# Attention in a two-layer trunk: the values attended in two passes with the halves of v side by side, and five lower weight halves made by accumulating DMAs

## The reference, cut to what matters

```python
q, k, v = jnp.split(h @ w_qkv, 3, axis=-1)
# z = q.k / sqrt(64); mask: key strictly before query
log_keep = jnp.where(mask, -jax.nn.softplus(z), 0.0)
suffix = lax.cumsum(log_keep, axis=3, reverse=True) - log_keep
a = jnp.where(mask, jnp.exp(jax.nn.log_sigmoid(z) + suffix + log_rem[..., None]), 0.0)
acc = acc + jnp.einsum("bhts,bhsd->bhtd", a, vblk)      # "the values attended"
return acc @ w_o
```

## Time and profile before

| | us |
|---|---|
| three runs | 1867.5, 1869.03, 1880.59 |
| median | 1869.03 |
| profiled execution, its own time | 1876.87 |
| its span in the trace | 1875.1 |
| PE / DVE / ACT / POOL busy in the span | 1834.6 / 1413.6 / 916.7 / 489.2 |

### The profile page before, as it was taken

The page is one execution under the profiler, slowest core; times in us unless marked ns, Lnnn a source line. Parts: engine busy times, 40 slices in busy tenths (PEclk is TensorE's granted clock), DMA queues, the critical chain, the costliest instruction groups (busy, mean ns, idle before and its releaser), DMA issues.

```text
span 1875.1 us, 29407 instructions
## 1 busy us (share of the span) xinstructions
PE 1834.6 (98%) x11801; PEld 1644.6 (88%) x11801; DVE 1413.6 (75%) x1309; ACT 916.7 (49%) x1110; POOL 489.2 (26%) x383
## 2 busy tenths in 40 slices
PE   6999999999999999999999999999999999999998
PEld 6999988887789999888999988888888889999886
DVE  7789876589888888765798885654766698988753
ACT  6455543355275555444545453435555475454442
POOL 3343302200023443001443310321333233432021
PEclk8999999999999999999999999999999999999999
DMA  8787632232268886436787732232111287776321
GB/s 226 182 221 179 172 122 90 75 94 67 80 152 185 214 183 168 130 101 132 185 202 189 190 124 90 79 96 62 46 45 45 68 182 191 189 190 158 112 90 45
DMA packets 228826, 250.94 MB, mean 134 GB/s; under 512 B 7844, under 2 KB 196336, under 8 KB 228224
## 3 DMA queue, kind: packets, MB, share of 16 engines
q1 hardware_dynamic: 179232, 195.58, 33.4%
q0 software_dynamic: 49392, 54.08, 18.5%
q10 hardware_dynamic: 112, 0.03, 0.0%
HBM read 241.27 MB, written 2.10 MB: 130 GB/s over the span
## 4 chain that ended last, share of the span: by engine, by line
PE 81%; DVE 10%; issue 4%; ACT 2%; POOL 2%; DMA 1%; DVEq 0%; ACTq 0%; POOLq 0%
PE ps L604 36%; PE ps L400 13%; PE ps L401 13%; PE ps L402 13%; DVE y L1833 2%; DVE w_lo L1540 2%; PE ps L933 2%; PE ps L912 1%; PE ps L918 1%; DVE rinv L1530 1%; DVE w_lo L1511 1%; POOL chain L2163 1%; DVE hid L1593 1%; ACT w_hi L1035 1%; DMA hid<-hid 0%
## 5 line engine op out<-in xcount | busy, mean ns | idle before, releaser
L1540 DVE TENSOR_TENSOR w_lo<-stage,w_hi 128x1024 fp32r<-128x1024 f32 x264 | 384.2, 1467 | 31.4 <-ACT w_hi L1073 31.0
L604 PE MATMUL ps<-xs_hi,w_hi 128*128 128x256 f32 x2464 | 339.9, 279 | 11.8 <-ACT w_hi L1073 10.2
L604 PE MATMUL ps<-xs_hi,w_lo 128*128 128x256 f32 x2464 | 338.6, 279 | 6.8 <-DVE w_lo L1540 6.7
L604 PE MATMUL ps<-xs_lo,w_hi 128*128 128x256 f32 x2464 | 338.2, 279 | 2.8 <-DVE xs_lo L1751 2.2
L604 PEld LDWEIGHTS ps<-xs_hi,w_hi 128*128 128x128 f32 x2464 | 309.2, 189 | 15.0 <-issue 14.7
L604 PEld LDWEIGHTS ps<-xs_hi,w_lo 128*128 128x128 f32 x2464 | 308.3, 189 | 8.2 <-DVE w_lo L1540 8.2
L604 PEld LDWEIGHTS ps<-xs_lo,w_hi 128*128 128x128 f32 x2464 | 308.2, 188 | 3.8 <-DVE xs_lo L1751 2.8
L400 PE MATMUL ps<-xs_hi,w_hi 128*128 128x512 f32 x704 | 278.4, 395 | 0.0
L401 PE MATMUL ps<-xs_lo,w_hi 128*128 128x512 f32 x704 | 278.2, 395 | 0.0
L402 PE MATMUL ps<-xs_hi,w_lo 128*128 128x512 f32 x704 | 278.2, 395 | 0.0
L1673 DVE TENSOR_TENSOR xs_lo<-hid,xs_hi 128x1024 fp32r<-128x1024 f32 x88 | 110.5, 1256 | 177.5 <-ACT xs_hi L1192 177.4
(11 more groups left out here) (241 smaller groups left out, 2736.6 us busy)
## 6 DMA issues: line engine op xcount, KB each, us to landing
stage<-in_w_ffn_up_dram SPq DMA_DIRECT2D x88, 512.0 KB, 4.5
stage<-in_w_ffn_gate_dram SPq DMA_DIRECT2D x88, 512.0 KB, 5.2
stage<-in_w_ffn_down_dram SPq DMA_DIRECT2D x88, 512.0 KB, 3.8
chain<-in_w_ffn_gate_dram POOLq DMA_DIRECT2D x47, 512.0 KB, 6.2
stage<-in_w_ffn_gate_dram POOLq DMA_DIRECT2D x44, 512.0 KB, 8.3
chain<-in_w_ffn_up_dram SPq DMA_DIRECT2D x43, 512.0 KB, 7.1
stage<-in_w_qkv_dram SPq DMA_DIRECT2D x24, 512.0 KB, 4.8
stage<-in_w_in_ab_dram SPq DMA_DIRECT2D x16, 512.0 KB, 4.6
```

The source lines that it names most:

```text
L604: mm = pe.matmul(ps[:, bank + BANK_OF[item], t * HS:(t + 1) * HS], w[:, slot, (2 * k + t) * P:(2 * k + t + 1) * P], xs[:, PART_OF[item], k ...
L1540: dve.tensor_tensor(w_lo[:, slot, :], src, w_hi[:, slot, :].bitcast(F32), ALU.subtract).then_inc(item_lo_made, 1)
```

## The change

v is kept in one tensor `v_cat` in which the 64 upper and the 64 lower columns of a head lie side by side. attend takes these 128 columns as its weights and makes two passes, one with prob_hi and one with prob_lo. Rows 0 to 63 of bank 7 then hold the product with the upper half of v, rows 64 to 127 that with the lower half (the product lower by lower, which was left out before, comes with it). ACT moves one half to the rows of the other in `sq` (`o_moved`), and DVE adds the two into `o_att` (`add_o`, which now signals `o_copied`), behind prob_lo in its iteration.

For chunks 7 to 11 DVE's subtraction goes. In even iterations 2 to 10 ACT writes -w_hi to `w_lo` (`negate`), and in odd iterations 3 to 11 POOL issues a DMA that adds `stage` to it in SBUF (`add_lower`, 1 MB). `lower_ready` is the wait for a chunk's lower half, by either way. `project` makes its 24 matmuls in the order of the three parts, and asks for the lower half ahead of the third. Line numbers behind @@ are those of the kernel before and after; split_v on ACT and the waits of the first projections change in the same manner as what is shown.

```diff
@@ -83,6 +83,9 @@
+ADDED = tuple(range(C_ATT + 7, C_ATT + 12))
 PE_TILE = CT - 1
...
@@ -187,8 +190,7 @@
             o_att = sb("o_att", [P, DT, S], scope=att_scope)
-            v_hi = sb("v_hi", [P, TT, D], F32R, att_scope)
-            v_lo = sb("v_lo", [P, TT, D], F32R, att_scope)
+            v_cat = sb("v_cat", [P, TT, HEADS, 2, DH], F32R, att_scope)
         mixer_scope.close()
...
@@ -335,6 +340,13 @@
+        def lower_ready(engine, c):
...
+            if c in ADDED:
+                engine.wait_ge(w_lo_added[c % 2], 16 * sum(1 for other in ADDED if other <= c and other % 2 == c % 2))
+            else:
+                engine.wait_ge(w_lo_made, sum(1 for other in range(c + 1) if other not in ADDED))
...
@@ -390,6 +402,11 @@
+        def o_split(j):
...
+            both = v_cat[:, :, 2 * j:2 * j + 2].rearrange("p t h a c -> p t (h a c)")
+            return both[:, :, 0:P], both[:, :, P:2 * P]
...
@@ -422,7 +439,7 @@
                     sp.wait_ge(w_hi_made, c - 1)
-                    sp.wait_ge(w_lo_made, c - 1)
+                    lower_ready(sp, c - 2)
...
@@ -872,14 +889,17 @@
                 slot = (n // 2) % 2
-                pe.wait_ge(w_lo_made, c0 + 5 + n // 2)
+                pe.wait_ge(w_hi_made, c0 + 5 + n // 2)
                 if n == 2:
...
                     pe.wait_ge(proj_scaled, n)
-                for k in range(DT):
-                    mm = three(pe, ps[:, 6, :], *tile(slot, (n % 2) * DT + k), xg_hi[:, k, :], xg_lo[:, k, :],
-                               start=(k == 0), stop=(k == DT - 1))
+                for part in range(3):
+                    if part == 2:
+                        lower_ready(pe, c0 + 4 + n // 2)
+                    for k in range(DT):
+                        mm = pe.matmul(ps[:, 6, :], tile(slot, (n % 2) * DT + k)[part // 2], (xg_lo if part == 1 else xg_hi)[:, k, :],
+                                       start=(part == 0 and k == 0), stop=(part == 2 and k == DT - 1), skip_group_check=True)
...
@@ -922,28 +942,26 @@
-                j = h // 2
                 pe.wait_ge(prob_hi_made, h + 1)
...
                     pe.wait_ge(o_copied, h)
-                for n, (v, part) in enumerate(((v_hi, prob_hi), (v_lo, prob_hi), (v_hi, prob_lo))):
-                    if n == 2:
+                for n, part in enumerate((prob_hi, prob_lo)):
+                    if n == 1:
                         pe.wait_ge(prob_lo_made, h + 1)
                     for b in range(TT):
-                        mm = pe.matmul(ps[:, 7, b * P:S], v[:, b, j * P:(j + 1) * P],
+                        mm = pe.matmul(ps[:, 7, b * P:S], v_cat[:, b, h].rearrange("p a c -> p (a c)"),
                                        part[:, KEY_OFF[b]:KEY_OFF[b] + KEY_COLS[b]], start=(n == 0 and b == 0),
-                                       stop=(n == 2 and b == TT - 1), skip_group_check=True)
+                                       stop=(n == 1 and b == TT - 1), skip_group_check=True)
                 mm.then_inc(att_summed, 1)
...
                 n, k0 = q // 4, 4 * (q // 8)
-                pe.wait_ge(w_lo_made, c0 + 13 + n)
+                lower_ready(pe, c0 + 12 + n)
                 for k in range(k_from, k_to):
                     pe.wait_ge(o_lo_made, k0 + k + 1)
-                    cols = slice((k0 + k) * P, (k0 + k + 1) * P)
                     mm = three(pe, ps[:, bank, :].rearrange("p (t c) -> p t c", t=TT), *tile(n % 2, 4 * k + q % 4),
-                               v_hi[:, :, cols], v_lo[:, :, cols], start=(k == 0), stop=(k == 3))
+                               *o_split(k0 + k), start=(k == 0), stop=(k == 3))
                 if k_to < 4:
...
@@ -1339,6 +1357,13 @@
             c0 = C_CONV
+            def negate(c):
...
+                slot = slot_of(c)
+                act.wait_ge(w_hi_made, c + 1)
+                act.activation(w_lo_c[:, slot, :], w_hi_c[:, slot, :].bitcast(F32), ACT.Copy,
+                               scale=-1.0).then_inc(w_neg_made, 1)
...
@@ -1441,8 +1466,7 @@
                 act.wait_ge(o_copied, 2 * j + 2)
-                act.activation(v_hi[:, :, j * P:(j + 1) * P], o_att[:, j, :].rearrange("p (t c) -> p t c", t=TT),
-                               ACT.Copy).then_inc(o_hi_made, 1)
+                act.activation(o_split(j)[0], o_att[:, j, :].rearrange("p (t c) -> p t c", t=TT), ACT.Copy).then_inc(o_hi_made, 1)
...
@@ -1472,14 +1496,16 @@
                     act.wait_ge(att_summed, h - 1)
-                    r = slice(DH * (h % 2), DH * (h % 2) + DH)
-                    act.activation(o_att[r, (h - 2) // 2, :], ps[r, 7, :], ACT.Copy).then_inc(o_copied, 1)
+                    r, other = slice(DH * (h % 2), DH * (h % 2) + DH), slice(DH - DH * (h % 2), P - DH * (h % 2))
+                    act.activation(sq[r, :], ps[other, 7, :], ACT.Copy).then_inc(o_moved, 1)
                 if h >= 3 and h % 2:
...
                     split_static(c0 + 14)
+                if h % 2 == 0 and 2 <= h <= 10:
+                    negate(c0 + 6 + h // 2)
             split_static(c0 + 15)
...
@@ -1988,9 +2014,9 @@
                     dve.wait_ge(v_hi_made, 4 * half + t + 1)
-                    cols = slice(half * 512, (half + 1) * 512)
-                    dve.scalar_tensor_tensor(v_lo[:, t, cols], ps[:, 4 - 4 * half + t, :], tok_rinv[:, t:t + 1],
-                                             v_hi[:, t, cols].bitcast(F32), ALU.mult,
+                    heads = slice(8 * half, 8 * half + 8)
+                    dve.scalar_tensor_tensor(v_cat[:, t, heads, 1], ps[:, 4 - 4 * half + t, :].rearrange("p (h c) -> p h c", h=8),
+                                             tok_rinv[:, t:t + 1], v_cat[:, t, heads, 0].bitcast(F32), ALU.mult,
                                              ALU.subtract).then_inc(v_lo_made, 1)
...
@@ -2017,9 +2043,15 @@
                 dve.wait_ge(o_hi_made, j + 1)
-                cols = slice(j * P, (j + 1) * P)
-                dve.tensor_tensor(v_lo[:, :, cols], o_att[:, j, :].rearrange("p (t c) -> p t c", t=TT),
-                                  v_hi[:, :, cols].bitcast(F32), ALU.subtract).then_inc(o_lo_made, 1)
+                o_hi, o_lo = o_split(j)
+                dve.tensor_tensor(o_lo, o_att[:, j, :].rearrange("p (t c) -> p t c", t=TT), o_hi.bitcast(F32),
+                                  ALU.subtract).then_inc(o_lo_made, 1)
...
+            def add_o(h):
...
+                r = slice(DH * (h % 2), DH * (h % 2) + DH)
+                dve.wait_ge(o_moved, h + 1)
+                dve.tensor_tensor(o_att[r, h // 2, :], ps[r, 7, :], sq[r, :], ALU.add).then_inc(o_copied, 1)
...
@@ -2040,7 +2072,7 @@
                     scale_proj(h + 2)
-                if h % 2 == 0 and h <= 14:
+                if h in (0, 12, 14):
                     split_static(c0 + 6 + h // 2)
...
@@ -2070,6 +2102,8 @@
                                       ALU.subtract).then_inc(prob_lo_made, 1)
+                if h >= 2:
+                    add_o(h - 2)
                 if h == HEADS:
...
@@ -2242,7 +2276,16 @@
+            def add_lower(*chunks):
...
+                for c in chunks:
+                    pool.wait_ge(w_neg_made, ADDED.index(c) + 1)
+                    pool.dma_start(w_lo_c[:, slot_of(c), :], stage_c[:, slot_of(c), :].bitcast(F32R),
+                                   accum_op=ALU.add).then_inc(w_lo_added[c % 2], 16)
...
             for h in range(HEADS + 1):
+                if h % 2 and 3 <= h <= 11:
+                    add_lower(C_ATT + 6 + (h - 1) // 2)
                 if h < HEADS:
```

More of the change, by code:

```diff
@@ L206, in trunk_kernel @@
         w_lo_made = sem("w_lo_made")
+        w_neg_made = sem("w_neg_made")
+        w_lo_added = [sem("w_lo_added0"), sem("w_lo_added1")]
         w_used = sem("w_used")
@@ L311, in trunk_kernel @@
         o_half_summed = sem("o_half_summed")
+        o_moved = sem("o_moved")
         o_copied = sem("o_copied")
@@ L462, in load_first @@
                     if n == 1:
-                        sp.wait_ge(w_lo_made, C_ATT - 1 + h)
+                        lower_ready(sp, C_ATT - 2 + h)
                     elif n == 3:
-                        sp.wait_ge(w_lo_made, CHUNKS - 1 + h)
+                        lower_ready(sp, CHUNKS - 2 + h)
                     elif n == 2:
@@ L857, in _ @@
             c0 = C_ATT
-            pe.wait_ge(w_lo_made, c0 + 1)
+            lower_ready(pe, c0)
             pair_chunk(0, (2, 3), NORM_ATT, True, NORM_ATT)
@@ L862, in _ @@
                 half, kh = n // 2, n % 2
-                pe.wait_ge(w_lo_made, c0 + 2 + n)
+                lower_ready(pe, c0 + 1 + n)
                 if n == 0:
@@ L1429, in split_v @@
                 for t in range(TT):
-                    act.activation(v_hi[:, t, half * 512:(half + 1) * 512], ps[:, 4 - 4 * half + t, :], ACT.Copy,
-                                   scale=tok_rinv[:, t:t + 1]).then_inc(v_hi_made, 1)
+                    act.activation(v_cat[:, t, 8 * half:8 * half + 8, 0], ps[:, 4 - 4 * half + t, :].rearrange("p (h c) -> p h c", h=8),
```

(1 more changed line is left out.)

## The result

The changed kernel took 1886.72 us in the median of 20 runs (1876.07 to 1899.7), the kernel before 1873.32 us in 20 runs taken beside them (1865.79 to 1885.96). The ratio is 1.0069, with a 95% interval of 1.0051 to 1.0087: about 13 us slower, 9.5 to 16.3. The forecast of 1874 with 4.9 us of loss had the sign; the time lies 1.7 us above its range. The profiled execution took 1890.0 us, its span 1888.3.

What follows compares the result with a forecast made beforehand. PE's passes were taken to set the pace. Against 10.2 us saved, waits left losses of 1.1 up to out_part(0), 3.2 at the end and 0.6 for the DMA: 4.9 on 1869.03, forecast 1874, range 1861 to 1885.

Steps and rivals of the forecast that it cites:

- the two waits that it named: In the attention loop, ACT's split_out and PE's attend wait for add_o: 12.18 us a head, where PE alone needs 11.78.
- T: Time at which scores(h) of an odd attention iteration ends and ACT starts its first step on them.
- The waits at attend: PE's attend may not overwrite bank 7 before add_o: 1.6 us at first, then about 0.9 every odd iteration.
- The end of the loop: Waits of 4.2 us at out_part(0), 2.45 at out_part(3), 2.5 more than 0.63 at parts 6 and 7, 0.65 at last tile.
- The 0.8 us that part 4 was to inherit: At out_part(4), 0.8 us inherited from the lateness at out_part(3).
- The clock: Rival: clock falls behind waits at out_part(0) to out_part(7), costing 1.7 us; one fall makes 1876, three 1879; chance 0.2.
- the waits eat the saving, clock unchanged: The forecast's main case: waits in the loop and at its end outweigh the 10.2 us saved, 4.9 lost; chance 0.38.
- The DMAs: Adding DMAs for chunks 7 to 11 land after 8.7 us, 0.7 too late for project; about 0.6 us lost in all.
- the late-landing rival: Adding DMA lands beyond 8 us: at 12 us 12 lost, 1881; at 14 us 17 lost, 1886; chance 0.12.
- The masks of prob: On POOL, 2.89 us in even and 1.61 in odd iterations; with 1.6 in both, about 3 us less loss.
- The base: 1869.03 us, the median of the kernel before, on which the loss of 4.9 was laid.
- The rival that PE stays the bound: In the loop, 10.2 us come through less 0.65: 1859.5; chance 0.12 for 5 us or more, 0.13 for less or nothing.

Runs made afterwards that it cites:

- the first kernel: The changed kernel with add_o moved on DVE from behind prob_lo to ahead of keep_hi (ahead of prob_hi from iteration 13); ratio to the kernel before 0.9966.
- the eighth: The changed kernel with add_o ahead of keep_hi, split_static ahead of split_out on ACT, and the last qk_f earlier on DVE; ratio to the kernel before 0.9976.
- the second: The changed kernel with split_out of a pair one iteration later on ACT and DVE; ratio to the kernel before 0.9989.
- the fifth: The changed kernel with split_static of the next chunk ahead of split_out on ACT, DVE unaltered; ratio to the kernel before 1.0005.

## Where the prediction was right, and the step that failed

*That PE is no longer the bound in the loop: right, by the two waits that it named.* In the terms of the prediction, with T = 1368.74: split_out started at T+12.9 (forecast T+12.7), ACT's next iteration at T+15.3 (15.2), keep at T+19.1 (19.1), add_o ended where qk_f starts, T+27.9 (27.9). add_o took 0.68 us with 0.60 to the next start (0.6). The waits at attend were 1.83 and three times 0.96 to 0.98 (1.6 and three times 0.9). One thing was not seen: ACT's first step of the next odd iteration was released by keep_lo, not by PE's scores, so that the loop closes over ACT, DVE and POOL in 24.73 us for two heads, not in 24.35 over PE. Over the three later pairs of heads that is 3 x 0.38 = 1.1 us. (The prediction's own sum gives waits of 0.8 and not 0.9: 48.7 us are 1.6 more than PE's 47.1 for four heads, that is for two waits.)

*The end of the loop: right in place, and nearly in size.* 4.28 us at part 0 (4.2), 2.50 at part 3 (2.45), 3.20 at part 7 (2.5 + 0.63), 0.74 ahead of the last tile (0.65). The 0.8 us that part 4 was to inherit did not come: in the changed kernel it starts 0.20 us behind the matmul ahead of it. The waits and the saving alone make a loss of 5.3 us in the changed kernel (11.3 - 6.0) and 5.7 in the one with idle matmuls; the forecast said 4.9. A part of this agreement is luck: 0.8 at part 4 and 0.6 for the DMA were forecast and did not come, while the loop over keep_lo (1.1) and some tenths at the other waits were not forecast and came.

*The clock: the step that failed.* The forecast's own words are "the waits eat the saving, clock unchanged". The prediction had the fall behind these waits as a rival with a chance of 0.2 and 1.7 us for each, and left it out of the forecast. It happened behind all three, cost 6.0 us in place of 5.1 (the first alone 2.75, since it lasted 6.7 us), and came again when the changed kernel was run again. The kernel with idle matmuls shows the cause and the size: with the same waits filled, no fall and 5.6 us less. The evidence was in the earlier trace rows: PE had been idle for 1.7 of 5 us there, and the clock fell; the waits that the prediction itself forecast were 2.5 to 4.2 us long, and should have had that price from the start.

*The DMAs: forecast 0.6 us, measured 0.1 or nothing.* The landing took 7.7 us in the median, below the 7.8 at which the prediction said it costs nothing, and 8.0 at the most, with PE waiting for none; the late-landing rival, which needed more than 8, fell. The Trainium skill ("DMA: Bandwidth & Descriptors", section "Anatomy of one DMA") gives an estimate of 4.4 us for this DMA; 7.7 measured, and 7.1 in the kernel with the DMAs alone, go against it again.

*The masks of prob.* They took 2.86 to 2.90 us in both parities, and both now lie beside keep_hi and keep_lo; the even iteration's prob_lo ended at T+27.4 all the same (27.3), so that the timetable was not moved by them. What shorter masks would give was not tried.

*The base.* The forecast laid its loss on 1869.03, the median of three runs; 20 runs give 1873.32, 4.3 us higher. Of the 12.7 us between forecast and result these are 4.3, the clock 6.0, the waits' excess 0.4 to 0.8; the rest, 1.6 to 2.0 us, is the difference between the median's loss (13.4) and the section's (11.3), within the interval of the ratio. The range, 1861 to 1885, allowed for one or two of these at once but not for all. Without the clock's 6.0 us the result would lie inside the range, but so it would without the base's 4.3: that the time lies 1.7 us outside does not tell by itself which term failed. The traces do, and in the ratio, where the base plays no part, the clock is the largest term.

*The rival that PE stays the bound* was false for this order and true for another: the 10.2 us are there in full once add_o, split_out, the last qk_f and two additions stand elsewhere.

## What to carry to other kernels

When an edit takes a step from the engine that bounds and puts a small one on another engine, don't price the step, price its place: 0.68 us behind prob_lo instead of ahead of keep_hi was 16 us of the section, the clock's part included. Write out which instruction now signals the semaphore, at what time of the iteration, and what is queued behind each waiter; that timetable held here to 0.3 us in the loop. Then give each new TensorE wait of the lengths seen here (1.8 to 4.3 us) a price beyond its length, for the clock behind it, by what the same trace shows behind idle time of that size; and where such a wait can't be removed, idle matmuls in it are worth a try (5.6 us here). And look at both kinds of waiter: with ACT's order alone changed the loop was cured and the end was not.

## What the runs showed of the hardware

The granted clock fell inside a stretch that was otherwise fully busy, at waits of 4.28 us (6.7 us at the lower level, 0.9 of them before PE resumed), 2.50 and 3.20 (3.4 us each); without the DMAs the same three waits gave 6.8 us each. Shorter waits went either way: behind 1.77 us in the first kernel it fell for 3.4 us, behind 1.75 us in the eighth it did not; in the second it fell behind 2.33 and not behind 2.85; in the fifth it fell at 3.35 (6.8 us) and 1.99 (3.4 us) and not at 1.31; and it fell behind none of the four waits at attend, the first of them 1.83 us. What decides between them stays open.

An accumulating DMA of 1 MB within SBUF took 7.1 to 8.6 us to landing in the nine runs that have it, with 1.03 us of POOL for the issue, and 9.0 in the fold of squares.
